# Samples' paged attention in steps between panels of another branch, memory keys and values first

## The chip, the cores and the metric

The kernel runs on one core of a Trainium2 chip. The metric is the device time of one launch in microseconds. Of several executions the median is given; one execution was also taken by the hardware profiler, and every duration of an instruction below is from it. The engines are named PE (TensorE, matmuls), DVE (VectorE), ACT (ScalarE), POOL (GpSimd) and SP (SyncE, which here issues nearly all transfers). TensorE's clock has two levels, 1.2 and 2.4 GHz; the granted clock of a stretch is given as a share of the upper one.

## The reference

One decoder layer runs on 512 new prompt tokens and on 8 samples of 8 tokens each, 576 columns in all. Three branches read the same normed input: differential attention, a spatial-gating MLP, and attention over memory tokens. Each is projected and gated, then they are summed.

```python
def _layer(x, l, past_k, past_v, mem_k, mem_v, ...):        # run for the prompt and for the samples
    h = _rmsnorm(x, g_attn)
    zq, zk, zv, zu, zs, zm, zg = split(h @ w_in)
    # differential attention: prompt over itself; each sample over its 512 cached and 8 new positions
    s = einsum('bqhcd,bkhcd->bchqk', q, k) * DA_DK ** -0.5 + bias[t5_bucket(dist)]
    p = softmax(where(dist >= 0, s, NEG_INF));  a = p[:, 0] - lam * p[:, 1]
    o_da = _rmsnorm(einsum('bhqk,bkhd->bqhd', a, v), subln_g) * (1 - lam_init)
    # spatial gating: vn = rmsnorm(s), mixed over positions within chunks of 128
    o_sg = u * (einsum('gts,bnsgd->bntgd', tril(sg_w), vn) + sg_b)
    # memory attention: 4 heads of 256 over 256 memory tokens
    o_mx = softmax(zm @ mem_k.T * MX_DH ** -0.5) @ mem_v
    merged = sum(sigmoid(zg[i]) * (o_i @ w_branch[i]) for i in range(3))
    x = x + merged @ w_out
    x = x + (silu(gate) * up) @ w_down;   return _rmsnorm(x)
```

For the prompt the memory keys and values are `rmsnorm(mem) @ w_mem_kv`, computed here and also returned; for the samples they come from a cache, as do the samples' keys and values of 512 past positions, in four pages each that a page table names.

## The kernel before

**Panels.** Every product with a weight matrix is cut into panels of 128 output rows. The weights lie in `w_stream` in the order of the panels. A panel takes 512 KB of weights, splits them into a high part (`w_hi`) and a rest (`w_lo`), and multiplies with activations that are split in the same way: for each of 8 tiles of the inner dimension hi·hi, hi·lo and lo·hi, in two halves of 288 columns, 48 matmuls in all. Four engines work on a panel. SP loads the weights into one of two slots of `w_raw` (`load_w`, L507). ACT makes `w_hi` (`split_hi`, L693 to 696), for which it waits until the panel two earlier in the same slot has been multiplied. DVE makes `w_lo` (`split_lo`, L1128 to 1130). TensorE multiplies (`panel`, L1789 to 1805, matmuls at L1798). ACT or DVE takes the accumulator away (`evacuate`, L698 to 702) before the slot's next panel. A panel whose output also has to lie with positions on the partitions is turned by TensorE afterwards (`turning`, `turn_tile`, L1822 and 1824).

**The order of the work.** It is written by hand. STAGES (L58) gives each stage its first panel number; each engine has a program of its own that goes through the stages in the same order, and semaphores tie them. Each engine executes its program strictly in order; SP's program, too, issues its transfers in order, and a wait in it holds all that stand behind. The stages are: q, k, v (8 panels each); the samples' paged attention; the prompt's attention; da_branch (16 panels: gate and output rows in turn); s and u (8 each) for the gating branch; sg_branch (16); zm (8, the memory queries); mk and mv (8 each on the 256 memory tokens); the samples' memory attention and the prompt's; mx_branch (16); w_out (8); up (22 pairs) and down (24).

**The samples' paged attention** (TensorE L1896 to 1942) treats one sample after another: `s_score` multiplies the queries with 4 pages of keys and the new keys (`k_pg`, `k_odd`); ACT and DVE form the probabilities; `s_turn_probs` turns them (L1908, 1909); `s_values` multiplies with 4 pages of values (`v_pg`) and the new values (`v_new`) (L1923); `s_combine` makes the difference of the two softmaxes and adds the heads' halves (L1934); DVE and ACT norm it; `s_turn` turns the result (L1942). SP's `load_keys_values` (L546) fetches the pages of later samples, each set when its buffer is free: there are two key buffers and one for values. Before it, SP reads the page numbers from memory into registers (L527).

**The gating branch.** The normed s stands turned with positions on partitions. POOL copies the 128 rows of a group into `s_slot`; `mix` (TensorE L2058 to 2068) multiplies them with the chunk weights `sg_w`, and for the samples with `sg_ws`, which SP fills with eight small transfers (L635). The mixes of groups 0 to 4 stand between the u panels, three behind the last.

**Memory.** mk and mv are made on the memory tokens, normed at that point. `kmT_new` and `vm_new` lie in the chip's memory, and are also returned. The cached pages of the samples come in pairs of 1 MB transfers.

## Time and profile before

| what | us |
|---|---|
| three executions | 1468.65, 1472.1, 1472.67 |
| their median | 1472.1 |
| the profiled execution | 1469.03 |
| its span on the core | 1466.9 |
| granted clock, mean of the span | 0.964 |

The stages of that execution, from its timeline (us from the start): q, k and v end at 188.8; samples' paged attention to 296.5; prompt attention to 385.2; da_branch, s and u to 609.2; sg_branch and zm to 764.6; mk and mv to 815.4; memory attention, the samples' to 853.8 and the prompt's to 895.2; mx_branch to 998.5; w_out to 1051.5; up to 1352; down to 1466.9.

Times in the rows are microseconds from the start of the span and durations in microseconds, or in nanoseconds where said. A row of a timeline groups like instructions that follow each other: start, the time from the start of the first to the end of the last, engine and line, operation, operands (out<-in), and what ended the idle time before. `128*32` is the part of the array that a matmul uses. In a chain of waits a row is one step back from the last instruction: what it waited for.

### The profile page before, as it was taken

To read this page: it belongs to the slowest core of one execution; us is meant where nothing else is said; L and a number is where in the kernel's file an instruction comes from. 1 tells how busy PE (TensorE), PEld (TensorE's weight loads), DVE (VectorE), ACT (ScalarE), POOL (GpSimd) and SP (SyncE) were. 2 spreads that over 40 slices of the span, in tenths; PEclk is the share of its full clock that TensorE was granted. 3 is DMA by queue.
4 is the path that set the end of the run, shared out by engine and by line. 5 is a ranking of instruction groups with operands and counts; after the bars stand their busy time and mean duration, and the time that the engine had idled before them with its cause. 6 is when DMAs were issued, how large, how long until landed. Compare 5 with 4: busy or idle time off the path is not lost.

```text
span 1466.9 us, 26769 instructions
## 1 busy us (share of the span) xinstructions
PE 1333.7 (91%) x9982; PEld 1243.6 (85%) x9982; DVE 685.3 (47%) x1204; ACT 552.9 (38%) x1025; POOL 61.3 (4%) x113
## 2 busy tenths in 40 slices
PE   4999956577899999999999789999899999999995
PEld 3999932245799999999999458999899999999995
DVE  6212321278622224533334333336788888874333
ACT  4222211157632223323334344334555555552221
POOL 2000010100100002100010000000000000000000
PEclk9999987879999999999999999999899999999997
DMA  5435479901024222123256821222222222222221
GB/s 198 130 93 204 134 235 288 309 19 55 16 85 125 93 101 96 58 86 117 85 201 189 326 116 44 84 74 87 86 87 86 104 96 86 88 70 87 88 98 64
DMA packets 78428, 171.89 MB, mean 117 GB/s; under 512 B 5565, under 2 KB 39613, under 8 KB 77350
## 3 DMA queue, kind: packets, MB, share of 16 engines
q1 hardware_dynamic: 76614, 164.08, 33.7%
q0 software_dynamic: 1760, 7.08, 1.4%
q8 instruction: 35, 0.57, 0.2%
q14 instruction: 19, 0.16, 0.0%
HBM read 161.68 MB, written 11.82 MB: 118 GB/s over the span
## 4 chain that ended last, share of the span: by engine, by line
PE 53%; issue 29%; DVE 8%; DMA 6%; ACT 2%; SPq 1%; POOL 0%; DVEq 0%; POOLq 0%; ACTq 0%
PE acc L1798 45%; DMA v_pg<-cache_v 2%; PE ps L1923 2%; DVE logit_p L1291 2%; DMA vm_pg<-mem_v 2%; DMA w_raw<-w_stream 1%; DVE a_p L1311 1%; PE acc L2173 1%; DVE a_p L1308 1%; DVE w_lo L1130 1%; ACT w_hi L696 1%; PE ps L1987 1%; DMA b_sel<-bias_select 1%; PE ps L1822 1%; PE acc L2153 0%
## 5 line engine op out<-in xcount | busy, mean ns | idle before, releaser
L1130 DVE TENSOR_TENSOR w_lo<-w_raw,w_hi 128x1024 fp32r<-128x1024 f32 x144 | 176.9, 1230 | 445.5 <-ACT w_hi L696 444.7
L1798 PE MATMUL acc<-h_hi,w_hi 128*128 128x288 f32 x1152 | 251.5, 300 | 4.7 <-DVE h_lo L1165 3.6
L1798 PE MATMUL acc<-h_lo,w_hi 128*128 128x288 f32 x1152 | 248.6, 297 | 0.0
L1798 PE MATMUL acc<-h_hi,w_lo 128*128 128x288 f32 x1152 | 248.5, 297 | 0.0
L696 ACT ACTIVATE w_hi<-w_raw 128x1024 fp32r<-128x1024 f32 x144 | 151.7, 1055 | 199.5 <-PE acc L1798 116.5
L1798 PEld LDWEIGHTS acc<-h_hi,w_hi 128*128 128x128 f32 x1152 | 185.1, 189 | 6.7 <-issue 3.4
L1798 PEld LDWEIGHTS acc<-h_hi,w_lo 128*128 128x128 f32 x1152 | 185.8, 189 | 0.0
L1798 PEld LDWEIGHTS acc<-h_lo,w_hi 128*128 128x128 f32 x1152 | 185.6, 189 | 0.0
L2226 PE MATMUL acc<-xs_hi,w_hi 128*128 128x288 f32 x352 | 105.4, 299 | 5.3 <-DVE w_lo L1502 4.2
L2226 PE MATMUL acc<-xs_lo,w_hi 128*128 128x288 f32 x352 | 105.5, 300 | 0.0
L2226 PE MATMUL acc<-xs_hi,w_lo 128*128 128x288 f32 x352 | 105.5, 300 | 0.0
L1798 PE MATMUL acc<-o_hi,w_hi 128*128 128x288 f32 x384 | 82.8, 297 | 2.0 <-ACT zmT L971 1.2
L1798 PE MATMUL acc<-o_lo,w_hi 128*128 128x288 f32 x384 | 82.6, 296 | 0.0
L1798 PE MATMUL acc<-o_hi,w_lo 128*128 128x288 f32 x384 | 82.5, 296 | 0.0
L2226 PE MATMUL acc<-xs_hi,w_lo_b 128*128 128x288 f32 x264 | 78.0, 296 | 0.0
L2226 PE MATMUL acc<-xs_lo,w_hi_b 128*128 128x288 f32 x264 | 77.8, 295 | 0.0
L2226 PE MATMUL acc<-xs_hi,w_hi_b 128*128 128x288 f32 x264 | 77.5, 294 | 0.0
L2253 PE MATMUL acc<-g_lo,w_hi 128*128 128x288 f32 x352 | 76.4, 299 | 0.0
L2226 PEld LDWEIGHTS acc<-xs_hi,w_hi 128*128 128x128 f32 x352 | 67.5, 192 | 5.7 <-DVE w_lo L1502 4.4
L2226 PEld LDWEIGHTS acc<-xs_lo,w_hi 128*128 128x128 f32 x352 | 67.5, 192 | 0.0
L1798 PE MATMUL acc<-m_hi,w_hi 128*128 128x256 f32 (+1 forms) x256 | 64.4, 292 | 3.2 <-DVE w_lo L1130 2.8
L2226 PEld LDWEIGHTS acc<-xs_hi,w_lo 128*128 128x128 f32 x352 | 67.2, 191 | 0.0
(297 smaller groups left out, 2369.1 us busy)
## 6 DMA issues: line engine op xcount, KB each, us to landing
w_raw<-w_stream SPq DMA_DIRECT2D x166, 512.0 KB, 3.5
v_pg<-cache_v SPq DMA_DIRECT2D x28, 512.0 KB, 5.9
w_raw_b<-w_stream SPq DMA_DIRECT2D x22, 512.0 KB, 4.2
k_pg<-cache_k SPq DMA_DIRECT2D x16, 512.0 KB, 5.9
k_odd<-cache_k SPq DMA_DIRECT2D x16, 512.0 KB, 6.4
km_pg<-mem_k SPq DMA_DIRECT2D x8, 1024.0 KB, 8.0
vm_pg<-mem_v SPq DMA_DIRECT2D x8, 1024.0 KB, 8.8
x_sb<-xT SPq DMA_DIRECT2D x8, 576.0 KB, 4.6
```

What stands on the lines that cost most here:

```text
L696: nc.scalar.activation(w_hi[:, u, :], w_raw[:, u, :], ACT.Copy).then_inc(w_hi_done, 1)
L1130: nc.vector.tensor_tensor(w_lo[:, u, :], w_raw[:, u, :], w_hi[:, u, :].bitcast(F32), ALU.subtract)\
L1291: last = nc.vector.tensor_tensor_reduce(out=logit_p[:, m, c, 0:w], in0=bank(4 + 2 * m + c)[:, 0:w], in1=bias_p[:, e, SEQ - w:SEQ], scale=1 ...
L1308: nc.vector.tensor_scalar(a_p[:, m, 0:w], logit_p[:, m, 1, 0:w], col(P_RC + 2 * m + 1), col(N_LAM), ALU.mult, ALU.mult).then_inc(p_a1, 1)
L1311: nc.vector.scalar_tensor_tensor(a_p[:, m, 0:w], logit_p[:, m, 0, 0:w], col(P_RC + 2 * m), a_p[:, m, 0:w], ALU.mult, ALU.add).then_inc(p_a, 1)
L1798: last = nc.tensor.matmul(acc[a][:, c, 0:n], w[:, u, k * P:(k + 1) * P], x[:, k0 + k, c * n:(c + 1) * n], start=start and k == 0 and t == ...
L1822: last = nc.tensor.transpose(bank(4 + u)[:, j * P:(j + 1) * P], turn[:, u, j * P:(j + 1) * P], ident)
L1923: last = nc.tensor.matmul(bank(4)[rows, 0:256], pT_s[:, j * P + 32 * g:j * P + 32 * g + 32], v, start=j == 0, stop=j == PAGES)
L1987: last = nc.tensor.matmul(bank(4 + 2 * m + c)[:, 0:w], qT[rows, 2 * hp + e, i * P:(i + 1) * P], kT[rows, 2 * hp + e, 0:w], start=True, sto ...
L2173: last = nc.tensor.matmul(bank(pv_bank(h) + f), vm_nat[:, m, h * MXD + f * P:h * MXD + (f + 1) * P], pT_m[:, m, :], start=m == 0, stop=m == 1)
L2226: last = nc.tensor.matmul(pair_bank(j, s), w[:, k * P:(k + 1) * P], x[:, k, X_KIND[j], :], start=BANK_START[j] and k == 0 and t == 0, stop ...
L2253: last = nc.tensor.matmul(acc[a][:, c, 0:HT], w[:, u, k * P:(k + 1) * P], x[:, c * HT:(c + 1) * HT], start=start and k == 0 and t == 0, st ...
```

## The change

Five things are moved. (1) mk and mv come first, on the memory tokens; SP loads the memory input and the weights of mk first, then x. The norm of x is done within them: its squares on ACT in mk, the statistics on TensorE behind mk4, the broadcast behind mk6, the scaling of h's tiles within mv. (2) s comes next, then q, k, v and u; the mixes stand behind each panel of k. (3) The pages' loads, the samples' scores, values and so on are steps of 24 panels, sg_branch and zm. Three panels go to a sample; `sample_step` (L2077) is called at the middle and at the end of each panel. (4) da_branch follows, and in it the samples' memory pages are fetched and the memory keys and values are loaded back (`kmT`, `vm_nat`) from the outputs that were stored early. (5) Memory attention, mx_branch and the rest follow as before.

```diff
 
-STAGES = (("q", 8), ("k", 8), ("v", 8), ("da_branch", 16), ("s", 8), ("u", 8), ("sg_branch", 16),
-          ("zm", 8), ("mk", 8), ("mv", 8), ("mx_branch", 16), ("w_out", 8), ("down", 24))
+STAGES = (("mk", 8), ("mv", 8), ("s", 8), ("q", 8), ("k", 8), ("v", 8), ("u", 8), ("sg_branch", 16), ("zm", 8),
+          ("da_branch", 16), ("mx_branch", 16), ("w_out", 8), ("down", 24))
...
@@ sync: the first loads
-            for c in range(4):
-                load_x(c, x_loaded[c])
+            for c in range(2):
+                sp.dma_start(m_x[:, 4 * c:4 * c + 4, :], memT[4 * c * P:(4 * c + 4) * P, :]
+                             .rearrange("(k p) n -> p k n", p=P)).then_inc(mem_loaded[c], 16)
                 if c == 0:
                     sp.dma_start(cst[:, :], consts).then_inc(cst_loaded, 16)
                     sp.dma_start(par[:, :], params).then_inc(cst_loaded, 16)
-            sp.dma_start(b_sel[:, :], bias_select).then_inc(sel_loaded, 16)
             for u in range(2):
                 load_w(u, u)
+            sp.dma_start(b_sel[:, :], bias_select).then_inc(sel_loaded, 16)
+            for c in range(4):
+                load_x(c, x_loaded[c])
             sp.dma_start(pages[:, :], page_table).then_inc(pages_loaded, 16)
+            for u in range(2):
+                load_w(2 + u, u)
...
@@ sync: what stands between weight loads
-            stream(2, FIRST["k"])
+            stream(4, FIRST["s"] + 2)
             sp.wait_ge(bias_skewed, 48)
-            key_pages(page_of(0), 0)
-            stream(FIRST["k"], FIRST["v"])
-            value_pages(page_of(0))
-            stream(FIRST["v"], FIRST["v"] + 4)
-            sp.wait_ge(n_lo, KT // 2)
-            sp.wait_ge(n_lo_odd, KT // 2)
-            key_pages(page_of(1), 1)
-            stream(FIRST["v"] + 4, FIRST["da_branch"] + 2)
-
-            third = page_of(2)
-            sp.wait_ge(s_scores, 1)
-            key_pages(third, 0)
-
-            sp.wait_ge(v_zero, 1)
-            load_new_values(0)
-            with sp.Fori(0, 2) as i:
-                load_keys_values(2 * i + 3, 2 * i + 1, 1)
-                load_keys_values(2 * i + 4, 2 * i + 2, 0)
...
+            sp.wait_ge(mm_done, FIRST["s"] + 1)
...
+            sp.dma_start(bias_s, bias_sd.rearrange("h c t k -> (h c t) k")).then_inc(bias_s_loaded, 16)
             sp.wait_ge(g_zero, 1)
             for b in range(NB):
                 sp.dma_start(sg_ws[b * TS:(b + 1) * TS, :, b * TS:(b + 1) * TS], sg_wT[0:TS, :, 0:TS],
                              allow_slow_non_contiguous=True).then_inc(sgs_loaded, 16)
+            stream(FIRST["s"] + 2, FIRST["v"] + 2)
+            sp.wait_ge(g_bias, KT)
+            key_pages(0)
+            stream(FIRST["v"] + 2, FIRST["u"] + 2)
...
+            sp.wait_ge(p_pv, 4 * HEADS)
+            sp.wait_ge(v_zero, 2)
+            value_pages(0)
+            key_pages(1)
+            for b in range(NB):
+                load_w(FIRST["sg_branch"] + 3 * b + 2, b % 2)
+                if b + 2 < NB:
+                    sp.wait_ge(s_scores, b + 1)
+                    key_pages(b + 2)
+                load_w(FIRST["sg_branch"] + 3 * b + 3, (b + 1) % 2)
+                load_w(FIRST["sg_branch"] + 3 * b + 4, b % 2)
+                if b + 1 < NB:
+                    sp.wait_ge(s_pv, b + 1)
+                    value_pages(b + 1)
...
+            stream(FIRST["da_branch"] + 2, FIRST["da_branch"] + 4)
+            sp.wait_ge(s_pv, NB)
+            sp.wait_ge(o_lo_done, 2 * KT)
             for e in range(2):
                 mem_keys(e, e)
+                stream(FIRST["da_branch"] + 4 + 4 * e, FIRST["da_branch"] + 6 + 4 * e)
                 mem_values(e, e)
-            stream(FIRST["mk"], FIRST["mx_branch"] + 2)
+                stream(FIRST["da_branch"] + 6 + 4 * e, FIRST["da_branch"] + 8 + 4 * e)
+            sp.wait_ge(early_stored, 48)
+            sp.dma_start(kmT[:, :, :], mkT_out.rearrange("(k p) n -> p k n", p=P)).then_inc(kv_loaded, 16)
+            sp.dma_start(vm_nat[:, :, :], mv_out.rearrange("(m p) n -> p m n", p=P)).then_inc(kv_loaded, 16)
+            stream(FIRST["da_branch"] + 12, FIRST["mx_branch"] + 2)
...
@@ scalar: memory keys and values with the norm of x between
+            for n in range(KT):
+                p, u = FIRST["mk"] + n, n % 2
+                evacuate(p, u, kmT_new[:, n, :], n=1)
+                split_hi(p + 2, u)
+                if n < 4:
+                    x_square(2 * n)
+                    x_square(2 * n + 1)
+                if n == 7:
+                    rms_out(1, T)
+            for n in range(KT):
+                p, u = FIRST["mv"] + n, n % 2
+                wait(act, turned, n - 1)
+                evacuate(p, u, mv_turn[:, u, :], n=1)
+                split_hi(p + 2, u)
+                x_hi_tile(n)
...
@@ vector: memory values
+            for n in range(KT):
+                split_lo(FIRST["mv"] + n + 2, n % 2)
+                x_scale(n)
+                if n % 2 == 0 and n:
+                    x_low(n - 2)
+                if n == KT - 1:
+                    x_low(KT - 2)
+                nat_copy(vm_new, n, n % 2, 0, MT)
...
@@ scalar: gating branch, memory queries, samples
+            s_exp_probs(0)
+            for c in range(24):
+                p, u, i = FIRST["sg_branch"] + c, c % 2, c // 2
+                if c < 16:
+                    if u == 0:
+                        act.wait_ge(acc_free[1], FIRST["sg_branch"] // 2 + i)
+                        evacuate(p, 0, halves(gate_s[:, :]), ACT.Sigmoid)
+                    else:
+                        act.wait_ge(mm_done, p + 1)
+                else:
+                    evacuate(p, u, halves(zmT[:, c - 16, :]), scale=MXD ** -0.5)
+                split_hi(p + 2, u)
+                b = c // 3
+                if c % 3 == 0:
+                    s_out_all(b)
+                elif c % 3 == 1:
+                    s_square(b)
+                else:
+                    s_output(b)
+                    if b + 1 < NB:
+                        s_exp_probs(b + 1)
...
@@ vector: the same panels
+            s_logits(0)
+            dve.wait_ge(v_zero, 2)
+            for c in range(24):
+                p, u, i, b = FIRST["sg_branch"] + c, c % 2, c // 2, c // 3
+                if c % 3 == 0:
+                    s_turned(b)
+                if c < 16 and u:
+                    dve.wait_ge(mm_done, p + 1)
+                    dve.wait_ge(acc_free[0], FIRST["sg_branch"] // 2 + i + 1)
+                    nc.vector.tensor_tensor(halves(merged[:, i, :]), acc_t(1), halves(gate_s[:, :]), ALU.mult)\
+                        .then_inc(acc_free[1], 1)
+                split_lo(p + 2, u)
+                if c % 3 == 0:
+                    s_coefs(b)
+                elif c % 3 == 1:
+                    s_norm(b)
+                elif b + 1 < NB:
+                    s_logits(b + 1)
...
@@ tensor: memory keys and values
+            for n in range(KT):
+                u = n % 2
+                slot_free("mk", n // 2, u)
+                panel(FIRST["mk"] + n, u, m_hi, m_lo, n=MEM, nc_=1, tile_ready=m_tile if n == 0 else None)
+                if n == 4:
+                    norm_stats(1, T)
+                if n == 6:
+                    norm_bcast(1, T)
+            pe.wait_ge(rms_ready, 2)
...
@@ tensor: keys with the mixes
+            for n in range(KT):
+                slot_free("k", n // 2, n % 2)
+                panel(FIRST["k"] + n, n % 2, h_hi, h_lo)
+                mix(n, n % 2)
...
@@ tensor: the samples' steps
+            def sample_step(g):
+
+                b, r = g // 6, g % 6
+                if r == 1:
+                    s_turn_probs(b)
+                elif r == 2:
+                    s_values(b)
+                elif r == 3:
+                    s_combine(b)
+                elif r == 5:
+                    s_turn(b)
+                    if b + 1 < NB:
+                        s_score(b + 1)
+
+            pe.wait_ge(p_logit, 4 * HEADS)
+            s_score(0)
+            pe.wait_ge(p_aT, 4 * HEADS)
+            for c in range(24):
+                p, u = FIRST["sg_branch"] + c, c % 2
+                if c == 1:
+                    pe.wait_ge(p_oout, HEADS)
+                slot_free("sg_branch", c // 2, u)
+                side = o_sg if c < 16 and u else (h_hi, h_lo)
+
+                def halfway():
+                    if c == 0:
+                        turn_output(HEADS - 1, 1)
+                    sample_step(2 * c)
+                if c == 1:
+                    pe.wait_ge(o_lo_done, KT)
+                panel(p, u, *side, halfway=halfway)
+                sample_step(2 * c + 1)
```

The order of instructions on the engines shows it at three places. The first is TensorE around the samples' attention; before it is one run of samples' work (a sample of the loop).

```order
L1896 MATMUL acc<-k_pg,q_blk 32x260 x16
L475 REGISTER_ALU
L1908 MATMUL acc<-cst,logit_s 128x128 x4
L1909 MATMUL acc<-cst,logit_s 8x128
L475 REGISTER_ALU
L1942 MATMUL ps<-cst,o_s 128x64
```

After it, the end of one sample's third panel, and the head of the next one (o_sg_hi and o_sg_lo are the gating branch's output, h the normed x):

```order
L1823 MATMUL acc<-h_hi,w_hi 128x288 x2
L1823 MATMUL acc<-h_lo,w_hi 128x288 x2
L1823 MATMUL acc<-h_hi,w_lo 128x288 x2
L2075 MATMUL ps<-cst,o_s 128x64
L2037 MATMUL ps<-k_odd,q_blk 32x260 x16
L1823 MATMUL acc<-o_sg_hi,w_hi 128x288 x2
L1823 MATMUL acc<-o_sg_lo,w_hi 128x288 x2
```

The turn and the score of the next sample, which stood among other steps of the samples, now stand between two panels.

The second is SP, where the pages are fetched. Before, a page's issues stand behind nothing but waits on the samples' own steps:

```order
L548 REGISTER_ALU
L532 ISA [waits s_scores]
L532 DMA k_odd<-cache_k 128x8x128
L532 ISA
L532 DMA k_odd<-cache_k 128x8x128
```

After, weight loads stand between the key pages of one sample and the value pages of another:

```order
L521 DMA k_even<-cache_k 128x8x128
L521 ISA
L521 DMA k_even<-cache_k 128x8x128
L497 DMA w_raw<-w_stream 128x1024 [waits w_lo_done] x2
L515 TENSOR_LOAD pages [waits s_pv]
L515 ISA x2
```

The page numbers (L515) are now read behind the wait on the samples' step, and weight loads follow the keys in one queue.

The third is ACT at the memory values. Before, in a turning stage such as v or mv:

```order
L702 ACTIVATE scaled<-acc 128x576 [waits mm_done]
L696 ACTIVATE w_hi<-w_raw 128x1024 [waits mm_done,w_loaded0]
L702 ACTIVATE scaled<-acc 128x576 [waits mm_done]
L696 ACTIVATE w_hi<-w_raw 128x1024 [waits mm_done,w_loaded1]
```

After, at the first panels of mv, with `mv_turn` the panel's output, `h_hi` a tile of the normed x:

```order
L683 ACTIVATE rms_b<-ps 128x512 [waits bcast_mm]
L684 ACTIVATE rms_b<-ps 128x64
L669 ACTIVATE mv_turn<-acc 128x256 [waits mm_done]
L663 ACTIVATE w_hi<-w_raw 128x1024 [waits mm_done,w_loaded0]
L732 ACTIVATE h_hi<-scaled 128x576 [waits n_scaled]
L669 ACTIVATE mv_turn<-acc 128x256 [waits mm_done]
L663 ACTIVATE w_hi<-w_raw 128x1024 [waits mm_done,w_loaded1]
```

A tile of h has come into each panel's row of evacuation and split.

## Rows read from the trace of the kernel before

**Rows 1.** The page's first part: busy us, share of span, instructions of each engine.

```profile
PE 1333.7 (91%) x9982; PEld 1243.6 (85%) x9982; DVE 685.3 (47%) x1204; ACT 552.9 (38%) x1025; POOL 61.3 (4%) x113
```

**Rows 2.** Windows of start, samples' stage, memory panels: stretch us, busy, PEclk, DMA, GB/s.

```profile
0.00:36.80 36.80, 16.96 (x62) 12.55 (x62) 22.85 (x36) 15.33 (x25) 9.59 (x12) 1.00 0.58 198
188.90:297.00 108.10, 61.06 (x665) 30.18 (x664) 22.03 (x69) 15.87 (x49) 11.16 (x37) 0.78 0.86 282
764.60:815.40 50.80, 47.36 (x396) 45.91 (x398) 22.48 (x23) 22.80 (x34) 1.40 (x3) 1.00 0.57 176
```

**Rows 3.** Chain of waits in the samples' stage: start us, us, what.

```profile
213.70 7.98 DMA v_pg<-cache_v
```

**Rows 4.** Chain of waits in the gating branch.

```profile
609.22 115.40 PE acc L1798 x864
```

**Rows 5.** TensorE timeline, samples' stage: start, us, engine line, op, tile, operands, idle.

```profile
188.84 1.96 PE L1896 MATMUL acc<-k_pg,q_blk 128*32 128x260 f32 x32
...
190.73 0.42 PEld L1822 LDWEIGHTS ps<-cst,scaled 128*128 128x128 f32 x4 [0.42 <-issue]
...
290.40 0.66 PE L1908 MATMUL acc<-cst,logit_s 128*128 128x128 f32 x4
290.89 0.27 PE L1909 MATMUL acc<-cst,logit_s 128*8 128x128 f32 x1
292.19 0.27 PE L1942 MATMUL ps<-cst,o_s 64*128 64x64 f32 x1 [1.02 <-DVE o_s L1239]
292.98 1.93 PE L1923 MATMUL ps<-v_pg,pT_s 128*32 128x256 f32 x32 [0.52 <-DVE pT_s L1246]
294.73 0.61 PE L1923 MATMUL ps<-v_new,pT_s 128*32 128x256 f32 x8
295.90 0.62 PE L1934 MATMUL ps<-o_all,coef_s 128*64 128x128 f32 x4 [0.55 <-issue]
296.45 0.49 PE L1987 MATMUL ps<-kT,qT 64*128 64x128 f32 x4
```

**Rows 6.** Timeline of SP's DMA issues for two samples' pages.

```profile
240.65 1.92 SPq L538 DMA_DIRECT2D v_pg<-cache_v  x4
242.76 0.33 SPq L544 DMA_DIRECT2D v_new<-vs_out  x1
248.60 4.16 SPq L532 DMA_DIRECT2D k_pg<-cache_k  x4
```

**Rows 7.** The page's DMA issues: count, KB each, us to landing.

```profile
v_pg<-cache_v SPq DMA_DIRECT2D x28, 512.0 KB, 5.9
...
k_odd<-cache_k SPq DMA_DIRECT2D x16, 512.0 KB, 6.4
...
w_raw<-w_stream SPq DMA_DIRECT2D x166, 512.0 KB, 3.5
```

**Rows 8.** Timeline of VectorE and ScalarE in the norm at the start.

```profile
31.17 0.81 DVE L1159 SCALAR_TENSOR_TENSOR gate<-x_sb,par,rms_b 128x576 f32<-128x576 f32 x1
...
32.01 0.69 ACT L724 ACTIVATE h_hi<-gate 128x576 fp32r<-128x576 f32 x1
```

**Rows 9.** The page's costliest groups: total busy us, mean ns of one.

```profile
L1130 DVE TENSOR_TENSOR w_lo<-w_raw,w_hi 128x1024 fp32r<-128x1024 f32 x144 | 176.9, 1230 | 445.5 <-ACT w_hi L696 444.7
...
L696 ACT ACTIVATE w_hi<-w_raw 128x1024 fp32r<-128x1024 f32 x144 | 151.7, 1055 | 199.5 <-PE acc L1798 116.5
```

**Rows 10.** Timeline of SP at the start.

```profile
18.98 0.69 SPq L575 DMA_DIRECT2D bias_pd<-line_d  x1
```

**Rows 11.** Transfers of the weights' slot (w_raw) in the first 110 us.

```profile
DMA to landing us min/median/max: 3.4/3.7/13.0
```

**Rows 12.** Timeline of SP after the prompt's attention.

```profile
468.24 5.87 SPq L635 DMA_DIRECT2D sg_ws<-sg_wT  x8
```

**Rows 13.** TensorE timeline, mixes of two panels of u.

```profile
578.19 1.05 PE L2064 MATMUL ps<-sg_w,s_slot 128*128 x8
...
586.03 1.05 PE L2064 MATMUL ps<-sg_w,s_slot 128*128 x8
```

More of the change, by code:

```diff
@@ new lines, in _, with o_sg_hi @@
+            act.wait_ge(g_ss, 1)
+            with act.Fori(0, 4) as i:
+                for u in range(2):
+                    p = FIRST["k"] + 2 * i + u
+                    evacuate(p, u, halves(kT[:, bass.ds(2 * i + u, 1), :].rearrange("p a n -> p (a n)")))
+                    split_hi(p + 2, u)
+            turning("v", 2 * KT)
+            def o_sg_hi(n):
+                act.wait_ge(g_out, n + 1)
+                nc.scalar.activation(o_sg[0][:, n, :], mixT[:, n, :], ACT.Copy).then_inc(o_hi_done, 1)
@@ L1825, in turn_tile, with turning @@
                 last.then_inc(turned, 1)
-            def turning(stage, x_hi, x_lo, count, nt=QT + 1, **kw):
+            def turning(stage, x_hi, x_lo, count, nt=QT + 1, turn=turn, first_tile=None, before_turn=None, **kw):
                 def body(i):
@@ L2034, in _, with s_score @@
                 p_body(hp, hp == HEADS // 2 - 1)
-            def branch(stage, split, before_output=None):
+            def s_score(b):
+                e = b % 2
+                pe.wait_ge(k_loaded[e], 16 * PAGES * (b // 2 + 1))
+                pe.wait_ge(s_q, 3 * (b + 1))
+                wait(pe, s_logit, b)
+                for lane in range(2):
+                    for c in range(2):
+                        for g in range(4):
+                            h, rows = 2 * g + lane, slice(32 * g, 32 * g + 32)
+                            last = nc.tensor.matmul(bank(4 + c)[rows, 0:HK], q_blk[:, h, :],
+                                                    k_slot[e][:, h, c * HK:(c + 1) * HK],
+                                                    start=lane == 0, stop=lane == 1)
+                last.then_inc(s_scores, 1)
@@ L2038, in o_tile, with branch @@
+            def branch(stage, o, split, before_output=None):
                 def o_tile(k):
```

953 lines of the change are left out of this document (416 added, 537 removed).

## The prediction

> **What bounds the kernel now.** I read the page's busy times first. TensorE (PE) is busy for 91% of the span and no other engine for over 47% [rows 1], so time can only come from stretches in which TensorE waits or works slowly, and they are few. The windows show them [rows 2]: the samples' paged attention, 188.84 to 296.45, has TensorE busy for 61 of 108 us at a mean granted clock of 0.78 with the DMA engines at 0.86; the start has 17 of 37. The chain of waits inside the stage says what ends last there: the landing of a page of values, 7.98 us and its like for each sample [rows 3]. That stage is bound by 33.5 MB of page traffic, not by arithmetic. Elsewhere the chain is TensorE alone: from 609.22 it runs 18 panels in 115.40 us, 6.41 each, with nothing between [rows 4]. During such a panel the DMA engines carry one 0.5 MB load, so there is room for the pages beside panels. The change goes for just this: the pages move under 24 panels that have TensorE full.
>
> **The stage that goes.** From the first score at 188.84 to the first prompt score at 296.45 are 107.6 us [rows 5]; the turn of v's last panel inside them (0.66 for its first piece at 190.7) stays. **−107.0**.
>
> **What comes back as TensorE work.** At the full clock a sample costs: score 1.96 (32 matmuls), turning the probabilities 0.66 + 0.27, values 1.93 + 0.61, combine 0.62, turning the output 0.27, together 6.32 [rows 5]. Rows overlap at their ends by 0.05 to 0.18 (1.93 from 292.98 ends after 294.73), so I take 6.0. The eight samples cost **+48**. The bounds: 5.6 if all overlap, 6.3 if none, 45 to 50. TensorE executes it all in its own path; only waits can be hidden.
>
> **Does the rest of a sample fit under its three panels?** The period of a sample is 3 × 6.42 + 6.0 = 25.3 us. In it SP fetches eight pages and three weights of 0.52 MB, 5.8 MB. The windows show 282 GB/s in the samples' stage as it stands [rows 2], so that is 20 us of 25.3. The order of issue counts too. In the steady state the weights of panel 3b+3 are issued behind the four pages of keys of sample b+2: four issues take 4.16 us and a key page lands after 6.4 [rows 6, 7]. Counted from the wait on the score of sample b, reading four page numbers (2.75: SP reads eight between the end of an issue at 243.09 and the next at 248.60 [rows 6]), 4.16, and a load behind pages make about 14 us, and the split of that weight is wanted at about 16. That is 2 us to spare, and I book **0**. If the cover fails, each sample costs what the load is late.
>
> **The start.** Today the first panel of q begins about 31.3, as the first tiles of h are ready (0.81 on DVE and 0.69 on ScalarE a tile [rows 8]), and mk and mv cost 50.8 later on [rows 2], their rate set by the supply of weights: load 3.5, split 1.055, low part 1.23 [rows 7, 9]. Put together, 82.1 us are gone before s. Now mk begins at about 19, on the memory's smaller norm, but its third weight waits behind the first loads and the 2 MB transfer of the bias line, issued at 18.98 today [rows 10]; the worst landing of a weight in the first 110 us was 13.0 against a median of 3.7 [rows 11]. I put panel mk2's weight at about 39. Then the norm of x (squares on ScalarE in mk, statistics behind mk4, broadcast behind mk6) is on the path, since TensorE waits for it before mv. In mv, ScalarE works per panel an evacuation, a split (1.055) and a tile of h (0.69), DVE a low part (1.23) and a scaled tile (0.81) in one chain, 4.2 us against 3.1 of matmuls. s begins at about 90.8. **+9**; from +2, if the bias transfer does not hold the weights, to +15.
>
> **Stalls at the new borders.** These follow from the queues; each is a wait which the trace of before does not show, so I bound each by rows.
> (1) SP waits for the first panel of s and then issues twelve small transfers ahead of the weights of s2; sg_ws alone takes 5.87 [rows 12], the four others some 0.4 each, in all 7.4. The load lands 3.5 later, splits take 1.055 + 1.23: 13.5 us after s0 ends, where s1 with its turn ends at 6.95. **+6.5**. Between 0, if SP were let go a panel earlier, and 8.
> (2) Weights v2 stand behind the wait for the eighth mix's bias, the four page reads and the four key issues of sample 0 (2.75 + 4.16) and land behind the keys (6.4): ready at 16.9 into v against 13.4 for the end of v1. **+3.5**, from 0 to 6.
> (3) Entering the 24 panels SP waits until the last head's values are done, then for the memset of the new values' tile, which itself comes after TensorE's turn halfway of the first panel; only then do 4 value pages go out (1.92 of issue, 5.9 to land), 4 key pages, and behind them the weights of the third panel. The first values are 4.4 late, the third panel's weights a further 5.0, and the next weights, which hold ScalarE's queue ahead of a sample's square, 1.6. **+11**, from 4 to 15: these overlap if one load's delay is the other's cover.
> (4) Prompt attention starts with logits whose vector work stands behind the last u panel's product and split: **+1** net of the slow start that it has today. The memory stage's first step waits for the last product and sum on DVE: **+1**.
>
> **What else goes.** The mixes move from u to k, 8 in either case: 586.03 − 578.19 = 7.85 for a panel and its mix against 6.41 without, so 1.43 each [rows 13], unchanged. Today the last three stand behind the last panel of u with waits: from the end of the fifth mix, about 601.7 by that spacing, to 609.22 [rows 4] are 7.5 us for at most 4 × 1.43. **−1.8**. The pages of the first two samples' memory keys and values are loaded ahead in both versions, now between da_branch's weights, and the samples' memory attention that follows is the same: **0**, from −5 if the earlier loads shorten it. The two reloads of memory keys and values (2 MB, through DRAM) ride in panels that have 3 us of slack a load: 0.
>
> **Sum.** −107.0 + 48 + 9 + 6.5 + 3.5 + 11 + 2 − 1.8 = −28.8. The profiled execution took 1469.0, so 1440.2; the median of the three runs is 3 above it, and I leave that 3 in the range. **Forecast 1440.**
>
> **The clock.** The samples' stage runs at a mean of 0.78 of 2.4 GHz today, between the two levels, with TensorE busy a little over half of it; the mk and mv panels show 1.00 [rows 2]. Under panels with no gaps I expect 1.00, and the durations of rows 5, from the last samples, are the shorter of those that the stage shows. That is in the 6.0.
>
> **Rivals.**
> (A) The borders are covered. None of (1) to (3) shows, as TensorE's own queue and the two weight slots take them up: 1440.2 − 21 = 1419. For it: panels have 3 us of slack each. Against: SP's queue is in order, and the issues behind the wait are there to be counted. 0.14.
> (B) Changing the shape of the tile costs a drain at each border. A sample puts in 128*32, 128*128, 128*64 and 64*128 tiles between panels of 128*128. Today, at the change from 128*32 to 128*128 at 190.73 the weight load had sat idle for 0.42 [rows 5], which I take as the most a border costs, and half of it as the least. Eight borders a sample, 64 in all, at 0.2 to 0.42 add 13 to 27: 1453 to 1467. Against: a mix (128*128 and 64*128 tiles) costs 1.43 for 1.05 and some 0.4 of matmuls, so that border is free. The Trainium skill, page "TensorEngine Tiling (Array Packing)", says under its key properties of tiling modes that changing the mode, not merely the tile, drains the engine; by it this rival holds, and the mixes here speak against it. 0.12.
> (C) The vector and scalar chain of a sample does not fit between its steps. From probabilities to values DVE and ScalarE have half a panel, 3.2 us, and both are in order, with a split of 1.055 and 1.23 in front [rows 9]. If each sample waits 3 us, +24: 1464. 0.08.
> (D) Slower than before. The weights of panel 3b+3 stand behind four key pages with the others' packets on the same 16 engines. They are 2 us to the good if the pages land in 6.4 [rows 7]. A weight load that lands after 13.0, as one did under such traffic [rows 11], is late by some 6 a sample, which makes 1488 with 8 samples; the sign turns where each sample loses 3.6 us (28.8 / 8), that is when the landing takes 5.6 us more than the 6.4. 1475 to 1494. 0.06.
>
> **How the numbers follow.** The forecast case has 0.60, (A) 0.14, (B) 0.12, (C) 0.08, (D) 0.06. The range takes in the forecast's own bounds and (A), and the nearer half of (B): 1418 to 1460. It leaves out (C), (D) and the dearer half of (B). A change of 0.3%, 4.4 us, is about what a measurement of this kernel can tell; the main case, (A), (B) and most of (C) lie below 1467.7: faster 0.92. Within 0.3%: 0.03. Slower, which is (D) in the main: 0.05.
>
> **What would show it.** The windows of the 24 panels: 24 × 6.42 + 48 + 11 = 213 us at a granted clock of 1.00. The chain there names weight loads and pages at its entry and nothing but panels after; a split of weights that waits for a load at every third panel means (D); an idle before the probabilities' turn or the values that ends on DVE or ScalarE at each sample means (C); score steps of over 1.96 with PE weight loads idle at the shape's change mean (B). s0 begins at 90.8; panel s2 starts 6.5 late with SP's small issues before its load; v2 starts 3.5 late. If the clock fell in the 24 panels, or if the memory stage gained from its earlier pages by more than 5, the forecast is wrong outside its terms.

## The result, and the profile after

The changed kernel took 1459.4 us in the median of four executions (1458.17 to 1460.80), against 1472.4 for the kernel before, timed beside it: a ratio of 0.9917, with a 95% interval of 0.9898 to 0.9936. It is faster, by 13 us. The forecast was 1440, so more than half of the expected gain is missing. The profiled execution took 1459.37 with a span of 1457.6, 9.3 less than the span before.

Of the page, these lines answer to [rows 1] and add the granted clock and the busy share of the DMA engines, in tenths, in 40 slices of 36.4 us.

```profile
PE 1334.3 (92%) x9982; PEld 1247.9 (86%) x9982; DVE 679.2 (47%) x1204; ACT 552.6 (38%) x1028; POOL 57.1 (4%) x98
...
PEclk9898999989999899999999799999999999999998
DMA  6344222334200386763352731222222322222221
```

TensorE is busy as long as before and the matmuls are as many. The share rose only by what the span shrank. The clock dips in single slices, and these name the places to look at: 36 to 73 us (mk), 109 to 146 (s2), 291 to 328 (v2), 474 to 510 (the entry of the 24 panels) and 802 to 838 (memory attention). The last slice dips too, as it did before.

The ledger by stage is made from TensorE's timelines of both executions. A stage reaches from its first matmul to the next stage's first. The first panel on the normed x (q0 before, s0 after) is counted to the start, and the eight plain panels that are left over for q are q1 to q7 and s0 before, q0 to q7 after.

| stage | before | after | difference | forecast |
|---|---|---|---|---|
| start, first panel on x, memory keys and values | 88.5 | 103.1 | +14.6 | +9 |
| the other seven panels of s | 48.6 | 61.8 | +13.2 | +6.5 |
| v | 55.1 | 66.2 | +11.0 | +3.5 |
| q, k, u with the mixes | 167.4 | 166.5 | −1.0 | −1.8 |
| samples' stage alone | 107.6 | none | −107.6 | −107.0 |
| prompt attention | 88.7 | 89.0 | +0.3 | +1 |
| the 24 panels | 154.6 | 215.7 | +61.1 | +48 and +11 |
| da_branch | 103.9 | 102.7 | −1.3 | 0 |
| memory attention to the end | 652.4 | 652.7 | +0.3 | +1 |

The differences add up to the 9.3 of the spans but for rounding. The stage that went and the panels that took it in came out as forecast. Four terms of loss came out larger: 5.6 at the start, 6.7 in s, 7.5 in v, 2.1 at the entry of the 24 panels.

The windows of those places, with the columns of [rows 2]: s1's end, the wait ahead of s2, s2 itself, the wait ahead of v2, v2, and then one sample's period in the 24 panels.

```profile
109.70:120.60 10.90, 0.54 (x5) 0.28 (x3) 1.25 (x2) 2.33 (x3) 1.75 (x2) 0.63 0.83 313
120.60:129.80 9.20, 9.16 (x50) 9.16 (x51) 1.90 (x3) 0.20 (x1) 0.00 (x0) 0.69 0.34 116
...
292.40:301.10 8.70, 0.57 (x6) 0.30 (x5) 1.28 (x2) 2.37 (x3) 0.00 (x0) 0.76 0.76 241
301.10:310.50 9.40, 9.40 (x50) 9.40 (x51) 1.86 (x3) 0.17 (x1) 0.00 (x0) 0.68 0.34 113
...
527.00:552.30 25.30, 25.30 (x231) 22.48 (x227) 7.22 (x14) 7.69 (x13) 2.08 (x5) 1.00 0.74 249
```

Before s2 and before v2 TensorE does next to nothing for 10.9 and 8.7 us. Then the panel itself takes 9.2 and 9.4 at a clock of 0.69 and 0.68, where its like takes 6.65. A sample's period has TensorE busy throughout at 1.00, with the DMA engines at 0.74.

The clock was low at other places too. These are the windows of mk4 (behind a gap of 7.7 us), mk7 (behind one of 4.1), the first values (behind 5.6) and the third of the 24 panels (behind 4.1):

```profile
43.67:48.50 4.83, 4.83 (x26) 4.83 (x26) 3.85 (x5) 2.11 (x4) 0.00 (x0) 0.57 0.54 174
59.40:63.40 4.00, 3.99 (x26) 3.79 (x25) 0.00 (x0) 0.00 (x0) 0.00 (x0) 0.75 0.40 135
504.80:508.50 3.70, 3.70 (x36) 1.99 (x40) 0.00 (x0) 0.00 (x0) 0.00 (x0) 0.50 1.14 307
516.47:524.17 7.70, 7.70 (x49) 7.46 (x48) 1.23 (x1) 1.31 (x3) 1.18 (x2) 0.85 1.07 365
```

Against their like at 1.00 they took 1.9, 0.9, 1.7 and 1.0 us more.

The chain of waits through one steady sample (start, us, what) answers to [rows 5]:

```profile
550.24 0.20 PE ps L2075
550.45 1.89 PE ps L2037 x32
552.34 6.60 PE acc L1823 x48
558.94 0.44 PE ps L2048 x4
559.38 0.11 PE ps L2049
559.49 3.21 PE acc L1823 x24
562.69 2.29 PE ps L2060 x40
564.99 3.40 PE acc L1823 x24
568.38 0.58 PE ps L2069 x4
568.96 6.59 PE acc L1823 x48
```

Nothing but TensorE stands in it. The next turn comes at 575.56, 25.32 later. The steps add up to 5.51 and the three panels to 19.80, 0.6 more than three of 6.40.

### The profile page after: what moved, and what is told of

It reads as the page before. It is cut to its first block, busy times and chain, and to the rows that moved or that the text cites. A ratio compares the mean times of both kernels' runs of the same rounds, so it can differ in the third digit from the quotient of the medians.

```text
span 1457.6 us, 26106 instructions
## 1 busy us (share of the span) xinstructions
PE 1334.3 (92%) x9982; PEld 1247.9 (86%) x9982; DVE 679.2 (47%) x1204; ACT 552.6 (38%) x1028; POOL 57.1 (4%) x98
## 4 chain that ended last, share of the span: by engine, by line
PE 52%; issue 30%; DVE 8%; DMA 3%; SPq 3%; ACT 2%; POOL 1%; DVEq 0%; POOLq 0%; ACTq 0%
PE acc L1823 44%; DVE logit_p L1337 2%; DMA w_raw<-w_stream 1%; DVE w_lo L1119 1%; ACT w_hi L663 1%; DVE a_p L1357 1%; PE ps L2060 1%; PE ps L2037 1%; PE acc L2199 1%; DVE a_p L1354 1%; SPq L521 1%; SPq L515 1%; DMA vm_pg<-mem_v 1%; DMA b_sel<-bias_select 1%; DMA km_pg<-mem_k 1%
## 5 line engine op out<-in xcount | busy, mean ns | idle before, releaser
L1823 PE MATMUL acc<-h_hi,w_hi 128*128 128x288 f32 x1152 | 255.4, 303 | 20.3 <-DVE w_lo L1119 18.5
L1823 PE MATMUL acc<-m_hi,w_hi 128*128 128x256 f32 (+1 forms) x256 | 67.7, 305 | 15.6 <-DVE w_lo L1119 11.1
L2280 PE MATMUL acc<-g_hi_main,w_hi 128*128 128x288 f32 x304 | 65.6, 297 | 0.0
L1823 PE MATMUL acc<-m_lo,w_hi 128*128 128x256 f32 (+1 forms) x256 | 65.6, 297 | 0.0
L1823 PE MATMUL acc<-m_hi,w_lo 128*128 128x256 f32 (+1 forms) x256 | 65.5, 297 | 0.0
```

The source lines that it names most:

```text
L1823: last = nc.tensor.matmul(acc[a][:, c, 0:n], w[:, u, k * P:(k + 1) * P], x[:, k0 + k, c * n:(c + 1) * n], start=start and k == 0 and t == ...
L2280: last = nc.tensor.matmul(acc[a][:, c, 0:HT], w[:, u, k * P:(k + 1) * P], x[:, c * HT:(c + 1) * HT], start=start and k == 0 and t == 0, st ...
```

## The experiments

Every kernel was timed beside the kernel before; 1459.4 is the changed kernel's median. Stages which no edit touches differ from execution to execution: the stretch from u7's end to the first gating panel took 89.9 to 94.2 us in the eleven profiles of the changed kernel and its variants. So the effect of an edit is read at its place, and the total is given beside it.

**Weights of s2 early.**

```diff
-            stream(4, FIRST["s"] + 2)
+            stream(4, FIRST["s"] + 4)
...
-            stream(FIRST["s"] + 2, FIRST["v"] + 2)
+            stream(FIRST["s"] + 4, FIRST["v"] + 2)
```

> One edit to the changed kernel: the weights of s2 and s3 are issued ahead of SP's wait for panel s0 and of the twelve small transfers that follow it. My theory (queue): the 10.6 us in which TensorE waited before s2, and the 2.5 us by which s2 then ran longer than its 6.65 (9.17, at a granted clock of 0.69), both come from those weights standing behind the small transfers. Then s2 starts 0.3 behind s1 and takes 6.65: 1459.4 - 13.1 = 1446.3. Rival (traffic): the small transfers and the bias table fill the DMA engines there whatever the order, so the wait only moves to s4, whose weights now stand behind them: 1455 to 1459.

Measured: 1445.84 us (ratio 0.9839, 0.9821 to 0.9856), 13.5 less. SP's timeline of the changed kernel shows the queue that was in the way (start, us of issuing), and the window of s2 in the edited kernel shows the panel at its normal length:

```profile
103.18 0.34 SPq L565 DMA_DIRECT2D norm_b<-sg_norm  x1
103.56 0.63 SPq L566 DMA_DIRECT2D sgb_b<-sg_bias  x1
104.24 1.23 SPq L567 DMA_DIRECT2D sg_w<-sg_wT  x1
105.51 1.43 SPq L568 DMA_DIRECT2D ssum<-bias_sd  x1
106.98 5.88 SPq L571 DMA_DIRECT2D sg_ws<-sg_wT  x8
113.23 0.88 SPq L497 DMA_DIRECT2D w_raw<-w_stream  x2
```

```profile
110.30:117.00 6.70, 6.70 (x53) 6.70 (x52) 2.10 (x3) 1.45 (x2) 1.10 (x1) 1.00 1.04 397
```

The small transfers hold SP for 9.7 us in which not a byte of weights is asked for. In the edited kernel SP asks at 95.6, and TensorE goes from s1 to s2 without a break. The DMA engines are full there, and s4 is not late all the same, so the traffic rival falls.

**Weights of v2 early.**

```diff
-            stream(FIRST["s"] + 2, FIRST["v"] + 2)
+            stream(FIRST["s"] + 2, FIRST["v"] + 4)
             sp.wait_ge(g_bias, KT)
             key_pages(0)
-            stream(FIRST["v"] + 2, FIRST["u"] + 2)
+            stream(FIRST["v"] + 4, FIRST["u"] + 2)
```

> One edit to the changed kernel: the weights of v2 and v3 are issued ahead of SP's wait for the eighth mix and of the first sample's key pages. My theory (queue): the 8.4 us of waiting before v2 and the 2.7 by which v2 ran long go: 1459.4 - 11.1 = 1448.3. Rival (traffic): v4's weights, which now stand behind the key pages, are late in their turn, since the pages and the store of the keys compete for the same DMA engines there: 3 to 8 us come back at v4, 1451 to 1456.

Measured: 1450.87 (ratio 0.9863, 0.9846 to 0.9879), 8.5 less. In its trace v takes 55.1 us again instead of 66.2, the 11.1 of the theory, and v4 starts 0.30 behind v3. What is missing in the total, 2.6, is found at the entry of the 24 panels, where the gap ahead of the fourth was 6.6 in that execution instead of 2.8. TensorE waited 2.7 instead of 0.7 for `o_s`, which VectorE makes behind the split of a weight, and the score that followed took 3.7 instead of 1.96, as at the lower clock. SP's four key issues ahead of that weight had taken 6.0 instead of 4.8. The edit does not touch that queue, so I count it to the differences between executions, without a proof.

**The entry of the 24 panels.**

```diff
-            stream(FIRST["u"] + 2, FIRST["sg_branch"] + 2)
+            stream(FIRST["u"] + 2, FIRST["sg_branch"] + 4)
...
+                if b == 0:                      # in value_pages, ahead of the pages
+                    sp.wait_ge(p_pv, 4 * HEADS)
+                    sp.wait_ge(stored, 32)
+                    sp.wait_ge(vs_stored, 16)
...
+                if b == 0:                      # behind the pages, ahead of v_new
+                    sp.wait_ge(v_zero, 2)
...
-            sp.wait_ge(p_pv, 4 * HEADS)         # ahead of value_pages(0)
-            sp.wait_ge(v_zero, 2)
...
             for b in range(NB):
-                load_w(FIRST["sg_branch"] + 3 * b + 2, b % 2)
                 if b + 2 < NB:
                     sp.wait_ge(s_scores, b + 1)
                     key_pages(b + 2)
-                load_w(FIRST["sg_branch"] + 3 * b + 3, (b + 1) % 2)
                 load_w(FIRST["sg_branch"] + 3 * b + 4, b % 2)
                 if b + 1 < NB:
                     sp.wait_ge(s_pv, b + 1)
                     value_pages(b + 1)
+                load_w(FIRST["sg_branch"] + 3 * b + 5, (b + 1) % 2)
+                load_w(FIRST["sg_branch"] + 3 * b + 6, b % 2)
```

> The entry of the 24 panels in the changed kernel: the weights of their third and fourth panel are issued before the prompt's attention ends, each later weight one step earlier, and the first value pages as soon as the last head's values are done, no longer behind the memset that waits for TensorE's turn. My theory (queue): the 24 panels took 215.6 us where eight samples at the steady 25.31 take 202.5; the 13.1 us of difference (waits, and the low clock that follows them) go: 1446.3. Rival (chain): the first sample's probabilities, made behind the prompt's last work on VectorE and ScalarE, are the later end, and 5 to 8 us of the difference stay: 1452 to 1454.

Measured: 1446.67 (ratio 0.9845, 0.9829 to 0.9862), 12.7 less. The chain of waits there holds TensorE alone from the first score at 484.61 on, and from the first score to the first panel of da_branch are 202.9 us, eight steady samples but for 0.4: the rival of the vector chain falls.

A second kernel has the early weights without the early value pages:

> As the run of the entry, but the first value pages keep their wait for the memset; only the weights go out early. Theory (queue): of the 13.1 us the values' own wait stays, 4 us and a piece of low clock, so 1450 to 1452. Rival (weights alone count): equal to the run with both edits, 1446. Second rival: the weights do not matter, the pages do: 1456 or more.

Measured: 1454.47 (ratio 0.9892, 0.9875 to 0.9908). Of the 12.7 the weights give 4.9 and the first values 7.8; read at the place, from the first of the 24 panels to da_branch, they give 5.1 and 7.8. The values' wait was dearer than I wrote. In the changed kernel TensorE's timeline around them is:

```profile
498.77 0.43 PE L1823 MATMUL acc<-o_sg_hi,w_lo 128*128 128x288 f32 x2
...
504.79 3.64 PE L2060 MATMUL ps<-v_pg,pT_s 128*32 128x256 f32 x32 [5.59 <-DMA v_new<-vs_out]
508.18 0.82 PE L2060 MATMUL ps<-v_new,pT_s 128*32 128x256 f32 x8
```

5.59 of waiting, and then 3.64 for what takes 1.93 in [rows 5]: the low clock again (0.50 in the window above), 1.7 more. The wait was put at 4.4 in the prediction and the clock at nothing.

**The bias line's transfers later.** On top of the early weights of s2, the two transfers to `bias_sd` and the 2 MB one to `bias_pd` are issued behind the weights of s3, and `bias_s` is read ahead of q's weights.

```diff
-            sp.dma_start(bias_pd, ...)          # and two to bias_sd, ahead of stream(4, ...)
             stream(4, FIRST["s"] + 4)
+            sp.dma_start(bias_pd, ...)          # and two to bias_sd
...
+            stream(FIRST["s"] + 4, FIRST["q"])
+            sp.wait_ge(bias_skewed, 48)
+            sp.dma_start(bias_s, ...)
```

> On top of the run with s2's weights early (1445.8): the three transfers that spread the bias line through memory (2 MB and 2 x 130 KB) are issued behind the weights of s3 instead of ahead of those of mk4, and the samples' bias is read at the end of s. My theory: the 7.7 us between mk3 and mk4 end on a weight that took 11.1 to land behind the bias transfer, and go: 1445.8 - 7.7 = 1438. Rival: x's loads, which stand ahead too, or the statistics of x on ScalarE and VectorE, are as late, and only 2 to 4 us go: 1442 to 1444; and if the bias transfer now holds s4's weights, none is left.

Measured: 1452.53 (1445.34 to 1453.71; ratio 0.9863, 0.9829 to 0.9896), not less than the 1445.8 on which it builds. The forecast of 1438 failed, and the trace shows both its theory and the last clause of its rival. The 7.7 us between mk3 and mk4 are gone, and s begins at 86.8 instead of 95.6. But s3 is followed by 6.5 us of waiting for s4's weights, and s4 takes 8.1 instead of 6.65. SP's timeline names the mechanism:

```profile
92.86 0.69 SPq L559 DMA_DIRECT2D bias_pd<-line_d  x1
94.77 9.30 SPq L564 DMA_DIRECT2D norm_b<-sg_norm  x1
104.11 0.59 SPq L565 DMA_DIRECT2D sgb_b<-sg_bias  x1
```

The issue of `norm_b` takes 9.30 where it took 0.34 before. Right behind the big transfer SP itself stands still, and all that follows in its program is asked for later. What was won in mk is so given back in s: u0 begins only 0.9 earlier than in the base. The profiled execution is 5.7 longer than the base's all the same, by 2.7 in prompt attention, 2.4 in memory attention and smaller pieces, stages that the edit does not touch. One of the four executions took 1445.3; whether the rest is chance, these runs don't settle.

**h's tile one panel later in mv.**

```diff
                 split_hi(p + 2, u)
-                x_hi_tile(n)
+                if n:
+                    x_hi_tile(n - 1)
+            x_hi_tile(KT - 1)
```

> One edit to the changed kernel: in mv, ScalarE makes h's tile of a panel one panel later, so that it no longer waits for VectorE's scaled tile before the next evacuation and split. My theory: the chain split, low part, scaled tile, tile, evacuation sets mv's period of 3.97 us; without it the panels take 3.1 and 7 to 8 us go: 1452. Rival: the two weight slots set the period (load, split, low part: 6.06 for two panels where mv stood before), with ScalarE's extra tile in between, at 3.5 to 3.9 a panel: 1455 to 1458.

Measured: 1453.33 (ratio 0.9878, 0.9854 to 0.9903), 6.1 less. From mv2 to mv7 a panel now takes 3.23 instead of 3.97, and from mv2's start to s1's it is 5.0 us less. The chain was what set the period, but the gain at the place is less than the 7 to 8 of the theory; one panel still waits 0.8, behind a scaled tile that took VectorE 1.98 instead of 0.81.

**The statistics one panel earlier.**

```diff
-                if n == 7:                      # ScalarE, in mk
+                if n == 6:
                     rms_out(1, T)
...
-                if n == 5:                      # VectorE, in mk
+                if n == 4:
                     norm_stats(1, T)
```

> Two moves of one place in the changed kernel: VectorE makes the statistics of x one panel earlier (behind the low part of mk6's weights) and ScalarE copies the broadcast one panel earlier. My theory: the 4.1 us of waiting ahead of mk7 and the 2.0 ahead of mv0 are this chain, standing behind weight splits in the two queues, and 4 to 6 us go: 1454.5. Rival: it is hidden behind mv's own chain, since h's tiles are wanted only in s: no change, 1459.

Measured: 1454.09 (1450.53 to 1457.14; ratio 0.9893, 0.9870 to 0.9916), 5.3 less. mk7 follows mk6 after 0.83 instead of 4.12, and mv0 follows mk7 without the 2.02. From mk6's start to mv0's it is 6.4 less: the wait was on the path.

**TensorE kept busy in the wait ahead of s2.**

```diff
+            def busy():                         # TensorE, between s1 and s2
+                for _ in range(70):
+                    nc.tensor.matmul(acc[0][:, 0, 0:HT], h_hi[:, 0, 0:P], h_hi[:, 1, 0:HT], start=True, stop=True)
```

> The changed kernel with 70 matmuls of 128x288 added (their result is not used) in TensorE's wait ahead of s2. Nothing else is moved, so s2 still starts when its weights are there, 120.6. My theory of the clock: s2 took 9.17 instead of 6.65 because the engine had rested 10.6 us; kept busy, it takes 6.65 and the kernel 2.5 less: 1456.9. Rival: s2 is slow for another reason (the transfers beside it, as the DMA engines are at 0.83 there): it stays at 9.2 and the time at 1459.

Measured: 1456.57 (1454.62 to 1459.19; ratio 0.9898, 0.9878 to 0.9918), 2.8 less. The windows of the wait and of s2, to be held against those of the changed kernel above:

```profile
109.30:120.60 11.30, 9.77 (x76) 9.54 (x73) 1.23 (x2) 2.33 (x3) 1.75 (x2) 1.00 0.82 302
120.60:127.30 6.70, 6.65 (x50) 6.65 (x51) 1.91 (x3) 0.21 (x1) 0.00 (x0) 1.00 0.46 157
```

The wait is as long, since the weights come no sooner, and the transfers beside it are the same. But the clock stays at 1.00 and s2 takes 6.65. So the 2.5 us on top of the wait are the clock's, and not the transfers'. The reading rests on these windows. The profiled execution itself took 1459.19, its gain at s2 lost again in prompt attention and at the entry, and the intervals of the two kernels overlap, so the 2.8 of the medians is no proof by itself.

**Pages left out.**

```diff
-                for j in range(PAGES):          # key_pages
+                for j in range(PAGES if b < 2 else 0):
...
-                for j in range(PAGES):          # value_pages
+                for j in range(PAGES if b < 1 else 0):
```

The kernel leaves out the keys from the third sample on and the values from the second on, and TensorE's waits on loads that are left out are lowered to match; its samples' attention is computed on the wrong pages.

> The changed kernel without the loads of keys from the third sample on and of values from the second on (the scores and values are multiplied with the pages that are there; page numbers are still read): 52 of 64 page loads of 512 KB are gone. Theory: in the steady part of the 24 panels the pages are wholly under cover, so a sample keeps its 25.31 us; only the second entry load (keys of sample 2, ahead of the fourth panel's weights) is won, 0 to 5 us: 1454 to 1459. Rival: packets of the pages slow TensorE's operands or its weights, and 0.5 to 1 us a sample goes as well: 1447 to 1452.

Measured: 1460.32 (ratio 0.9936, 0.9918 to 0.9955), no gain: at the entry the 24 panels were 0.9 shorter in its trace. A sample's period in this kernel:

```profile
526.00:551.30 25.30, 25.30 (x228) 22.49 (x227) 7.92 (x14) 8.45 (x13) 2.70 (x5) 1.00 0.20 65
```

The DMA engines fell from 0.74 to 0.20 and TensorE's time is the same to 0.1 us. The pages, on which a stage of 107.6 us ended before, cost nothing under the steady panels, neither by late weights nor by any contention. What a sample costs there is its matmuls. At the entry the pages do count: the pair of runs above put 7.8 us on the first values.

**All edits together**, with the bias line in four pieces of two heads each, between the weight loads of s and q:

```diff
+            for g in range(HEADS // 2):
+                load_w(FIRST["s"] + 4 + 2 * g, 0)
+                sp.dma_start(bias_pd[2 * g:2 * g + 2], ...)
+                load_w(FIRST["s"] + 5 + 2 * g, 1)
```

> All edits together on the changed kernel: s2's, v2's and the 24 panels' weights early, the first value pages early, h's tile one panel later in mv, the statistics one panel earlier, and the bias line spread in four pieces of 512 KB between the weight loads of s and q. Theory (each stall has its own cause in a queue): the gains stand beside each other: 1459.4 - 13.1 (s2) - 9 to 11 (v2) - 13.1 (entry) - 15 to 20 (start: 8, 5 and 6 apart) = 1404 to 1409. Rival (what is won at one border comes back at the next, since the transfers then overlap): at most two thirds of it, 1420 to 1430.

Measured over five executions: 1408.51 us (1403.8 to 1411.96; ratio 0.9578, 0.9555 to 0.9601), 51 less than the changed kernel and 62 less than the one before. Its page:

```profile
PE 1324.0 (94%) x9982; PEld 1239.2 (88%) x9982; DVE 682.4 (49%) x1204; ACT 553.4 (39%) x1028; POOL 58.5 (4%) x98
```

The gains do stand beside each other, as forecast (1404 to 1409). TensorE's busy time fell by 10.3 with the same 9982 matmuls; the extra time at the low clock that the changed kernel's panels show behind waits adds up to 10.7 (1.9 + 0.9 + 2.5 + 2.7 + 1.7 + 1.0). A wait of 2.0 is left ahead of s5, where the issue of its weights took 6.3 right behind the first piece of the bias line. Ahead of mk5 is a gap of 2.6, in which TensorE waits 1.4 for the sum of x's squares and then makes the statistics.

## Why the prediction was wrong

**Right: what the change moves.** The view of what bounds the kernel held. The stage of 107.6 us went whole. A sample's period was forecast at 25.3 and is 25.32. The forecast of 6.0 a sample beside panels of 6.42 comes out at 25.32 − 3 × 6.40 = 6.1. The run without pages shows that the cover is complete in the steady part, so that the margin for the weights, which I put at 2 us, was used up at none of the last seven samples. Rivals (C) and (D) fall by this. (The 6 us a sample of (D) left out that margin; with it a landing of 13.0 is 4.6 late, and 1488 would be about 1477.)

**Right: the places of the stalls.** s2, v2 and the entry stall, each for the reason that was given, a weight load behind other issues in SP's queue. Three runs with nothing but the order and the waits of that queue changed took them away. Rival (A), the borders are covered, falls.

**Wrong: their sizes.** This is the step that failed, in the part on the new borders, with two terms in it. Of the 21.9 us too little cost, the clock behind waits is 10.7 over all places, and the time in SP's queue 4.2 at s2 and 4.8 at v2; the remaining 2.2 are mainly at the start.

The first is the clock. I counted each stall as its wait and booked the panel behind it at its normal length. In this kernel the panel behind a wait of 8 to 11 us begins at the lower of the clock's two levels (0.69 and 0.68 as a mean of the panel), which cost 2.5 (s2) and 2.7 (v2) more. Behind shorter waits it cost 1.7 and 1.0 at the entry (there the waits themselves were forecast at 11.0 and came to some 10, so the 2.1 too little are the clock's) and 1.9 and 0.9 in mk. The price is not fixed: in the profiles of the variants the same two panels took 8.1 to 9.4, 1.5 to 2.7 more than 6.65. That the extra time is the clock's was tested at s2 alone; at the other places it is read from the granted clock. The page had shown such a thing to me, the mean of 0.78 in the samples' stage, and I used it for what would be won there and not for what would be lost at the new waits. The Trainium skill, page "TensorE: Matmul & The Clock Gate", in its Part 1 on the clock gate, says that the throttled state is the default and that activity releases it. The run with the added matmuls agrees, 9.17 against 6.65; by that rule alone I could have added a term to every stall.

The second is the time in SP's queue and behind it. For s2 I took 7.4 of issuing and 3.5 of landing; it was 9.7 and 5.0, since three of the transfers that I put at 0.4 took 0.6 to 1.4, and the weights landed among them. For v2, SP came to read the page numbers 2.7 into v, reading four took 5.0 instead of 2.75 and the issues 5.25 instead of 4.16. (The terms that I wrote down add up to 13.2 and 15.6, where I used 13.5 and 16.9; the 0.3 and 1.3 have no source.) My durations came from other places of the trace, and the DMA engines stand at 0.83 and 0.76 in these waits. For the page numbers traffic is not the reason, or not alone: at 507.80 to 509.80, with the DMA engines as full, a read took 0.26 to 0.28. What made them slow at v2 stays open. The trace before had slow ones too, 0.87 to 1.40 each at 138 to 142, also in v, and I took mine from the samples' stage.

**Wrong: the start**, by 5.6 of 14.6. mk4's weights did wait for the bias transfer (11.1 us to land), and mv's chain was as forecast, 3.97 against 4.2 a panel. What was missing are the two gaps around the statistics of x, 4.1 ahead of mk7 and 2.0 ahead of mv0, and the low clock in mk4 and mk7, 2.8 together; 1.3 more is s0 itself, 7.9 instead of 6.65. Against these, mk4 began 1.5 earlier than by my path and the eight panels of mv took 29.8 instead of 33.6; together this leaves about 5 of the 5.6. I had written that the norm is on the path and gave it no price of its own; moving it a panel earlier took 6.4 away there.

**Rival (B)**, a drain at each change of the tile's shape: by its size it would have been 13 to 27 us. The three panels of a sample take 19.80 with the steps between them instead of 19.2, so the 0.6 are the most that eight borders add to the panels, under 0.1 each, 5 us in all; the steps' own rows, 5.51, are no longer than in [rows 5]. They are within the forecast's 6.0 to 6.3 a sample. What the Trainium skill says of a drain, on the page "TensorEngine Tiling (Array Packing)" under Key Properties, may be so, but these rows show it at a size that decides nothing.

The total of the terms: 5.6 + 6.7 + 7.5 + 2.1 is 21.9 too little cost, 2.4 too much was booked elsewhere (da_branch won 1.3), and 1440.2 + 19.5 is the 1459.7 that the profiled execution took, but for rounding. The median of the kernel before, 3 above its own profiled execution, makes the gain 13 rather than 9.7.

## What to carry to other kernels

When a step moves, write down for each queue what stands behind it, and give a wait of TensorE its own length and the price of the low clock after it; here, at s2, v2 and the first values, that was a fifth to a quarter of a stall. Issue the weights of the next two panels ahead of anything in the same queue that has to wait or that is long, where their slots are free. Moving the pages under full panels was worth 59 us (107.6 less eight times 6.1) and some 50 of them were given back, nearly all at the seams; mending these with nothing but order was worth 51 us.

## What the runs showed of the hardware that I had not expected

Issuing is not a fixed price. The same small transfer took SP 0.34 us, and 9.30 us right behind a 2 MB transfer between places in memory with many small pieces. A weight load took 6.34 right behind a quarter of that transfer, and 0.36 when it was issued 4.4 us after the whole of it. Reading a page number took 0.9 to 1.1 us at v2 and 0.27 at the entry of the 24 panels, beside empty and beside full DMA engines; why, no run shows.

The clock can be held. Matmuls without use, put in a wait, made the following panel 2.5 us shorter, with nothing else moved; the kernel's median fell by 2.8 us, which is not clear of its spread.

With eight changes of the tile's shape a sample, TensorE's panels lost at most 0.6 us to all of them together, and taking the DMA engines' share beside full panels from 0.74 to 0.20 changed their time by less than 0.1 in 25.3 us.
